# A decoder step on one core: page numbers looked up once per turn, and forget sums spread by two matmuls

## The reference, cut to what matters

```python
# one short-convolution layer (A), then one layer of attention with forget values (B), on
# x_prompt (1, 512, 1024) and x_sample (8, 8, 1024); 16 heads of 64
k, v, f = split(rmsnorm(h) @ kv_w)              # shared keys, values, forget gates
logf = log_sigmoid(f + f_bias)
F_p = cumsum(logf_prompt, axis=1)               # (512, 16): the forget sums of the prompt
# prompt: s = q k^T / 8 + F[query] - F[key], causal, softmax, times v
# samples: the keys and values of 2048 old positions come from 16 pages of 128 rows,
k_past = cache_k[page_table].reshape(8, 2048, 16, 64)
v_past = cache_v[page_table].reshape(8, 2048, 16, 64)
# and the 8 new ones follow; the same attention over past and new
y = x + (o * silu(z)) @ b_w_out
```

## Time and profile before

| | us |
|---|---|
| median of 3 runs | 965.42 |
| lowest and highest | 959.49 and 969.38 |
| the profiled execution's own time | 968.43 |
| its span, first to last instruction | 966.6 |
| busy: PE, DVE, ACT, POOL | 852.6, 557.5, 342.4, 217.2 |
| mean granted TensorE clock, of full speed | 0.959 |

### The profile page before, as it was taken

The page is one execution under the profiler, slowest core; times in us unless marked ns, Lnnn a source line. Parts: engine busy times, 40 slices in busy tenths (PEclk is TensorE's granted clock), DMA queues, the critical chain, the costliest instruction groups (busy, mean ns, idle before and its releaser), DMA issues.

```text
span 966.6 us, 23640 instructions
## 1 busy us (share of the span) xinstructions
PE 852.6 (88%) x8516; PEld 707.5 (73%) x8516; DVE 557.5 (58%) x1039; ACT 342.4 (35%) x728; POOL 217.2 (22%) x130
## 2 busy tenths in 40 slices
PE   3899999999998997988787888887888878877998
PEld 2899999999997996756555656565556555654998
DVE  4745655555336355568485584684856746836632
ACT  4233333333025444252451442524514415235210
POOL 2233333331211032221322213203222132121000
PEclk8899999999999999899998998998999989989999
DMA  6232233323536463688998988998989889896212
GB/s 202 67 87 70 82 87 87 87 84 93 163 90 230 145 195 92 214 313 270 325 334 244 399 292 304 378 275 317 331 256 401 282 282 387 277 357 223 89 44 99
DMA packets 148482, 206.65 MB, mean 214 GB/s; under 512 B 10527, under 2 KB 93136, under 8 KB 147266
## 3 DMA queue, kind: packets, MB, share of 16 engines
q1 hardware_dynamic: 138802, 199.40, 61.6%
q10 hardware_dynamic: 9088, 4.46, 1.5%
q0 software_dynamic: 528, 2.10, 0.8%
HBM read 195.29 MB, written 10.63 MB: 213 GB/s over the span
## 4 chain that ended last, share of the span: by engine, by line
PE 54%; SPq 24%; issue 10%; DVE 7%; DMA 4%; ACT 1%; POOL 0%; DVEq 0%; ACTq 0%; POOLq 0%
PE psum L1293 31%; SPq L379 11%; PE psum L1319 9%; SPq L388 8%; PE psum L1450 4%; PE psum L1263 3%; SPq L396 2%; PE psum L1557 2%; DMA page_ring<-in_cache_k 2%; DVE page_ring L1067 1%; DMA w_raw<-in_a_w_in 1%; DMA w_raw<-in_a_w_out 1%; PE psum L1490 1%; PE psum L1512 1%; PE psum L1367 1%
## 5 line engine op out<-in xcount | busy, mean ns | idle before, releaser
L1293 PE MATMUL psum<-xn_high,w_high 128*128 128x256 f32 x992 | 230.4, 314 | 45.2 <-DVE page_ring L1067 42.3
L1293 PEld LDWEIGHTS psum<-xn_high,w_high 128*128 128x128 f32 x992 | 167.8, 193 | 79.3 <-DVE page_ring L1067 45.8
L1293 PE MATMUL psum<-xn_low,w_high 128*128 128x256 f32 x992 | 216.0, 300 | 0.0
L1293 PE MATMUL psum<-xn_high,w_low 128*128 128x256 f32 x992 | 215.5, 299 | 0.0
L1067 DVE STREAM_TRANSPOSE page_ring<-page_ring 128x1024 f32<-128x1024 f32 x128 | 153.4, 1224 | 32.8 <-DMA page_ring<-in_cache_k 31.2
L1293 PEld LDWEIGHTS psum<-xn_low,w_high 128*128 128x128 f32 x992 | 170.5, 193 | 0.0
L1293 PEld LDWEIGHTS psum<-xn_high,w_low 128*128 128x128 f32 x992 | 170.4, 193 | 0.0
L551 POOL TENSOR_TENSOR w_raw<-w_raw,gains 128x1024 f32<-128x1024 f32 x32 | 61.6, 1927 | 275.3 <-DMA w_raw<-in_b_w_in 244.0
L913 DVE TENSOR_TENSOR w_low<-w_raw,w_high 128x1024 fp32r<-128x1024 f32 x32 | 54.1, 1692 | 74.5 <-ACT w_high L629 74.5
L1450 PE MATMUL psum<-page_ring,q_current 32*32 32x512 f32 x2048 | 84.1, 700 | 0.0
L528 POOL TENSOR_TENSOR w_raw<-w_raw,gains 128x1024 f32<-128x1024 f32 x30 | 60.8, 2027 | 89.6 <-DMA w_raw<-in_a_w_in 89.6
(11 more groups left out here) (243 smaller groups left out, 1429.8 us busy)
## 6 DMA issues: line engine op xcount, KB each, us to landing
page_ring<-in_cache_k SPq DMA_DIRECT2D x256, 256.0 KB, 4.1
page_ring<-in_cache_v SPq DMA_DIRECT2D x128, 512.0 KB, 6.5
w_raw<-in_a_w_in SPq DMA_DIRECT2D x32, 512.0 KB, 4.0
sample_scores<-suffix_scratch SPq DMA_DIRECT2D x8, 1024.0 KB, 9.6
w_raw<-in_b_w_in SPq DMA_DIRECT2D x16, 512.0 KB, 5.1
w_raw<-in_kv_w SPq DMA_DIRECT2D x16, 512.0 KB, 5.9
w_raw<-in_a_w_out SPq DMA_DIRECT2D x4, 1024.0 KB, 4.9
f_broad<-f_scratch SPq DMA_DIRECT2D x8, 512.0 KB, 4.1
```

The lines of the kernel that those rows point to most:

```text
L1293: mm = pe.matmul(PS[:, bank + h, 0:c.stop - c.start], w[:, k, :], x[:, k, c], start=(k == 0 and n == 0), stop=(k == KT - 1 and n == 2))
```

## The change

The diff has two parts.

1. SP reads the page numbers of a sample once: 16 calls of page_of at the head of a turn, kept in 16 registers, from which both halves of the keys and the values take their addresses. For that, the loop is cut in another place: its body is now "look up the pages of sample i + 1, load its keys, load its values", so that keys and values share the registers. The first sample's pages are looked up ahead of the loop. The order of the DMAs is otherwise kept, except that the last turn's new_bias load stands after the residual loads.
2. The broadcast DMA into f_broad is gone. PE opens each turn with two matmuls, [16 x 128] times [16 x 512] each: the weights (head_rows, SEL) are a row of the identity repeated in 128 columns, which picks one head of f_sum, and the result is that head's forget sums on all 128 partitions, in banks T0 and T1. ACT copies them to f_broad at the head of its turn. POOL makes SEL for the next turn (`select`). FT moves from f_broad's place to new_keys'. PE waits for POOL (b_sel) ahead of the two matmuls and for ACT (b_fb) ahead of past_scores(0); ACT waits for PE (b_fbp).

```diff
-        def load_keys(b, n, free=None):
-            pages = [page_of(b, 2 * (n % 8) + e) for e in range(2)]
+        def load_keys(pages, n, free=None):
             if free:
                 sp.wait_ge(*free)
             for e in range(2):
-                src = kpages[bass.ds(pages[e], 1), :, n // 8 * HALF_D:(n // 8 + 1) * HALF_D]
+                src = kpages[bass.ds(pages[2 * (n % 8) + e], 1), :, n // 8 * HALF_D:(n // 8 + 1) * HALF_D]
...
-        def load_values(b, n, free=None):
-            page = page_of(b, n)
-            if free:
-                sp.wait_ge(*free)
-            src = vpages[bass.ds(page, 1), :, :]
+        def load_values(pages, n):
+            src = vpages[bass.ds(pages[n], 1), :, :]
...
+        first = [page_of(0, n) for n in range(NPG)]
         sp.wait_ge(s_cs, H)
...
-        sp.dma_start(f_dram, FT[:, :]).then_inc(s_fst, 16)
+        sp.dma_start(f_dram[:, SEQ:TOK], FT[:, SEQ:TOK]).then_inc(s_fst, 16)
...
-        def heads(i, last):
-            sp.wait_ge(b_c0f, 4 * i)
-            sp.wait_ge(b_c1f, 4 * i)
-            src = f_dram[bass.ds(2 * i, 2), 0:SEQ].unsqueeze(0).to_broadcast([P, 2, SEQ])
-            sp.dma_start(FB[:, :, :], src).then_inc(b_fb, 16)
+        def values(pages, i, last):
             if not last:
                 sp.wait_ge(b_split, KT + 3 * i + 1)
                 load_w(wkv, (i + 1 + KT) * P, 0)
             for n in range(NPG):
-                load_values(i, n, (b_scored, 2 * i + n // 8 + 1) if n % 8 == 0 else None)
+                if n % 8 == 0:
+                    sp.wait_ge(b_scored, 2 * i + n // 8 + 1)
+                load_values(pages, n)
...
+        def next_turn(i, last):
+            pages = [page_of(i + 1, n) for n in range(NPG)]
             for n in range(NPG):
+                load_keys(pages, n, (b_used, NPG * i + n + 1))
                 if n == 8:
                     sp.wait_ge(b_t0, 8 * i + 4)
                     sp.wait_ge(b_t1, 8 * i + 4)
+                    load_suffix(i + 1)
+                if n == 13:
                     sp.wait_ge(b_split, KT + 3 * i + 5)
                     load_w(wqz, (i + 1 + KT) * P, 1)
+            values(pages, i + 1, last)
+        values(first, 0, False)
+        with sp.Fori(0, NB - 2) as i:
+            next_turn(i, False)
+        next_turn(NB - 2, True)
...
# POOL, once and then in every turn after the copy of the queries
+        def select(i):
+            rows2 = CT[0:H, bass.ds(C_ID + 2 * i, 2)].unsqueeze(2).to_broadcast([H, 2, P])
+            pool.tensor_copy(SEL[:, :, :], rows2).then_inc(b_sel, 1)
...
+                pool.wait_ge(b_fbp, i + 1)
+                select(i + 1)
# ACT, first in its turn
+            act.wait_ge(b_c0f, 4 * i)
+            act.wait_ge(b_c1f, 4 * i)
+            act.wait_ge(b_fbp, i + 1)
+            act.activation(FB[:, :, :], PS[:, T0:T0 + 2, :], ACT.Copy).then_inc(b_fb, 1)
# DVE
-            dve.wait_ge(b_fb, 16 * (i + 1))
+            dve.wait_ge(b_fb, i + 1)
# PE, first in its turn
+            pe.wait_ge(b_t0f, 8 * i)
+            pe.wait_ge(b_t1f, 8 * i)
+            pe.wait_ge(b_sel, i + 1)
+            for e in range(2):
+                mm = pe.matmul(PS[:, T0 + e, :], SEL[:, e, :], FT[:, 0:SEQ], start=True, stop=True)
+            mm.then_inc(b_fbp, 1)
             project(0, range(KT - 1))
             pe.wait_ge(b_qc, 16 * (i + 1))
-            pe.wait_ge(b_t0f, 8 * i)
-            pe.wait_ge(b_t1f, 8 * i)
+            pe.wait_ge(b_fb, i + 1)
```

More of the change, by code:

```diff
@@ L219, in build @@
     FL = place("f_log", [H, TOK], over=at["probs"])
-    FT = place("f_sum", [H, TOK], over=at["f_broad"])
+    FT = place("f_sum", [H, TOK], over=at["new_keys"])
+    SEL = place("head_rows", [H, 2, P], over=at["new_keys"] + 4 * TOK)
     SN = place("new_scores", [P, NB, NS], over=at["new_keys"])
@@ L271, in build @@
     b_fb, b_nbs, b_es, b_lp, b_sot = (
-        sem("f_broad_loaded"), sem("sample_bias"), sem("sample_exp"), sem("sample_sum"), sem("sample_out"))
+        sem("f_broad_ready"), sem("sample_bias"), sem("sample_exp"), sem("sample_sum"), sem("sample_out"))
     b_nbp, b_ep, b_pn, b_po, b_sz, b_gf, b_gh, b_gl = (
@@ L283, in build @@
         sem("gated_sl"), sem("past_weight"))
+    b_fbp, b_sel = sem("f_broad_made"), sem("head_rows_ready")
     s_hld = sem("h_loaded")
@@ L405, in _ @@
         sp.wait_ge(s_rows, 16 * 9)
+        first = [page_of(0, n) for n in range(NPG)]
         sp.wait_ge(s_cs, H)
         for n in range(2):
-            load_keys(0, n)
+            load_keys(first, n)
         for t in range(NT):
@@ L438, in _ @@
             if n < KT + 1:
-                load_keys(0, 5 + n)
+                load_keys(first, 5 + n)
             if n == KT:
                 sp.wait_ge(b_proj, 2)
-                load_keys(0, 14)
-                load_keys(0, 15)
+                load_keys(first, 14)
+                load_keys(first, 15)
         sp.wait_ge(s_fnr, 1)
@@ L462, in heads @@
                     load_w(wkv, (i + 1) * P, 1)
-            if last:
-                sp.wait_ge(b_split, KT + 3 * NB)
-                load_slab(wo_b, 0)
+        def next_turn(i, last):
+            pages = [page_of(i + 1, n) for n in range(NPG)]
             for n in range(NPG):
[L468 to L473, removed]
+                load_keys(pages, n, (b_used, NPG * i + n + 1))
                 if n == 8:
@@ L477, in heads @@
                     sp.wait_ge(b_t1, 8 * i + 4)
[L478 to L483, removed]
+                    load_suffix(i + 1)
+                if n == 13:
                     sp.wait_ge(b_split, KT + 3 * i + 5)
                     load_w(wqz, (i + 1 + KT) * P, 1)
-        with sp.Fori(0, NB - 1) as i:
-            heads(i, False)
-        heads(NB - 1, True)
+            values(pages, i + 1, last)
[3 more added lines that the diff above has]
+        next_turn(NB - 2, True)
+        sp.wait_ge(b_split, KT + 3 * NB)
+        load_slab(wo_b, 0)
+        for t in range(NT):
+            sp.wait_ge(b_used, NPG * (NB - 1) + t + 1)
+            sp.dma_start(X2[0:rows(t), t, :], h_dram[t * P:t * P + rows(t), :]).then_inc(s_hld, 16)
+        sp.wait_ge(b_t0, 8 * (NB - 1) + 4)
+        sp.wait_ge(b_t1, 8 * (NB - 1) + 4)
+        sp.dma_start(NBI[:, :, :].rearrange("p b n -> p (b n)"), table[:, C_NM:C_NM + NB * NS]).then_inc(b_nm, 16)
         sp.wait_ge(b_t1f, 8 * NB)
@@ L556, in _ @@
         pool.tensor_copy(QT[:, :], QF[:, 0, 0:SEQ]).then_inc(b_qt, 1)
+        def select(i):
+            rows2 = CT[0:H, bass.ds(C_ID + 2 * i, 2)].unsqueeze(2).to_broadcast([H, 2, P])
+            pool.tensor_copy(SEL[:, :, :], rows2).then_inc(b_sel, 1)
+        pool.wait_ge(s_st, 1)
+        select(0)
         def low_b(n, slot):
```

## The result

| | before | after |
|---|---|---|
| median, us | 962.45 (958.03 to 969.38) | 933.64 (930.4 to 946.28) |
| after / before, 95% interval | | 0.9699 [0.962, 0.9777] |
| span of the profiled execution, us | 966.6 | 944.4 |
| mean granted TensorE clock | 0.959 | 0.964 |

The kernel is 3% faster, by 29 us; I had forecast 40 (965 to 925).

What follows compares the result with a forecast made beforehand. SP's DMA issues and look-ups were taken to bound each turn, with PE next. Seven turns save 41.3 us and the last past_scores(1) 1.5, together 42.8 from 968.4: 925.6, called 925 us; range 917 to 944.

Steps and rivals of the forecast that it cites:

- The turn of 58.5 us: One past_scores(1) to the next: PE's 56.84 us without waits for keys, plus 1.7 for the new matmuls, makes 58.5.
- Seven turns: 450.8 - 7 x 58.5 = 41.3 us: Turns 0 to 6 together: 450.8 us measured before, each turn becoming 58.5, saves 41.3 us.
- The matmul pair: 1.7 taken: PE at the turn's head: two float32 matmuls of 512 columns add 1.6 to 1.8 us, taken as 1.7.
- ACT's copy at nothing: ACT's copy of the forget sums from PSUM, 1.06 us, falls near free time and costs nothing, at most 0.5 us.
- Rival D: PE waits for ACT's copy into f_broad, 1 us or so in each of 7 turns: 932 us. Chance 0.07.
- Look-ups at 0.58 us: SP's turn: each look-up costs 0.58 us; 48 a turn become 16, 27.8 us become 9.3, removing 18.5.
- These 21 us are the cover: PE frees the sixteen slots over 21.4 us, more slowly than SP issues, so SP's grouped look-ups are covered.
- The loop's end counted as moved, at no gain: SP's loop end, 3.8 us of issue, now stands between the values and the next sample's look-ups; no saving was counted.
- Rival A: Transfers bind next; the queue may run dry 6 to 7 us before slot 0's keys: turn 61 us, 944.6 us. Chance 0.2.
- Rivals B: SP stays the bound: the 1.16 us between slots is the queue's pace, only f_broad's issue goes: 963 us. Chance 0.04.
- C: Slower: holding 16 page numbers makes each DMA's address dearer; at 0.5 us each, turn 69, time 1000 us. Chance 0.03.
- The short waits ... come from DVE's softmax steps, which nothing here touches: PE's short waits inside the attention blocks come from DVE's softmax steps and stay in the 56.84 us turn.

Runs made afterwards that it cites:

- Experiment 4: The kernel after with f_sum and head_rows on 128 partitions, added ones zero, so the broadcast matmuls use 128 rows: 925.81 us, 0.9577 of before.
- Experiment 10: Experiment 4 with the 16 look-ups at the turn's head done twice, 9.3 us of SP more: 980.05 us, 1.0129 of before.
- experiment 3: The kernel after, unaltered, run again as the yardstick of its group: 937.76 us, 0.9626 of before.
- 2: The kernel after, with its matmuls and new loop cut, but a look-up ahead of each DMA, 48 a turn: 947.36 us, 0.9776 of before.
- 7: The kernel before with only the forget sums changed to matmuls, its old loop and 48 look-ups kept: 959.51 us, 0.9928 of before.
- 5: The kernel after with the 16-row matmul pair moved behind the first three eighths of the projection: 928.94 us, 0.96 of before.
- 1: The kernel after with f_broad by the DMA of before, so only the look-ups and the loop's new cut are changed: 926.78 us, 0.9572 of before.
- 6: The kernel after with POOL's two low parts waiting until DVE has done the softmax step beside which they ran: 917.81 us, 0.9502 of before.
- 8: The kernel after with both 128-row broadcast matmuls and POOL's low parts held until DVE's softmax steps are done: 918.47 us, 0.9415 of before.
- experiment 9: The kernel after with f_broad by the DMA of before and POOL's low parts held until DVE's softmax steps are done: 924.07 us, 0.9556 of before.

## Why the prediction was right, and where it was off

The range held the time (933.64 in 917 to 944), and so did the mechanism in the main: SP's issues bounded the turn, and now PE does. Which part of SP's work counted was off, and that the total came out within 9 us is partly luck, as errors of opposite sign stand in it.

- **The turn of 58.5 us: right at full clock.** 58.4 was measured. The step that failed is the multiplication by seven. "Seven turns: 450.8 - 7 x 58.5 = 41.3 us" took the clock of one turn for all; the profiled execution's seven took 433.6, 24 us above 7 x 58.5, all of it in turns at 0.89 and 0.94. Its own time is the longest of the four, so it overstates this: by the medians 8.6 us are missing. Against it stand the 4.3 us ahead of the turns, which I had not forecast. I had seen that the turn of 61.70 us, from which 56.84 came, was the only one shown that ran at 1.00 throughout, and should have kept a term for the fall.
- **What makes the falls long: 16 rows in the matmuls at the turn's head.** In none of the long falls do the matmuls start it. In the turn of the pair at 438.19 the clock falls some 2 us ahead of it, in the last attention block, behind the wait of 1.73 us, and it is back only at about 446.4:
```profile
434.00:435.80 1.80, 0.91 (x11) 0.56 (x14) 1.80 (x3) 0.52 (x3) 0.75 (x1) 1.00 1.06 328
435.80:438.10 2.30, 2.30 (x24) 0.63 (x16) 2.30 (x5) 2.10 (x9) 0.00 (x0) 0.56 1.01 198
...
446.80:450.00 3.20, 3.20 (x26) 3.20 (x26) 0.00 (x0) 0.00 (x0) 0.00 (x0) 1.00 1.11 341
```
Experiment 4 has the same fall, behind a wait of 1.64 us and 1.4 us ahead of its pair, and there, with 128 rows, the clock is back as the pair ends:
```profile
499.79 3.01 PE L1480 MATMUL psum<-f_sum,head_rows 128*128 128x512 f32 x4
498.30:500.60 2.30, 2.30 (x13) 0.89 (x14) 2.30 (x3) 2.08 (x10) 0.00 (x0) 0.54 1.15 287
...
502.20:510.00 7.80, 7.80 (x82) 6.85 (x81) 4.82 (x6) 1.03 (x1) 0.00 (x0) 1.00 1.02 319
```
Experiment 10, with 128 rows too, has one like it (the clock low from 708.0 to 711.5, the pair at 709.76). Ten low stretches of 10 us stand in the profiles with the 16-row pair at the head (three in after, four in experiment 3, two in 2, one in 7); in each the clock fell 1.6 to 3 us ahead of the pair, and the pair ran at the lower level (3.8 us); nine make the turns at 0.89. With 128 rows (4), another place (5), no pair (1) or POOL held off (6) none is over 4 us. (Before and experiments 8 to 10 have some of 7 us around past_scores(1), where PE waits for slots.) Seven of the nine turns come from two executions, the ones of 946.28 and 952.77 us, but the mean clocks of all executions say the same: 0.957 to 0.976 in the twelve of the changed kernel, 0.978 to 0.98 in five of six with 128 rows, 0.976 to 0.987 in all six with the other place. For the median it is only indicated: the intervals of experiments 3 and 4 overlap (0.9574 to 0.9678, 0.9525 to 0.9629).
- **The matmul pair: 1.7 taken, 1.91 measured** at the upper level. By my own row's most (0.91 for 576 columns) I should have stayed at 1.8.
- **ACT's copy at nothing: right.** ACT's timeline in after:
```profile
442.01 1.02 ACT L760 ACTIVATE f_broad<-psum 128x1024 f32<-128x1024 f32 x1 [1.73 <-PE psum L1479]
```
In this turn at the lower level ACT had crossed its loop's end and stood waiting. In the turn at the upper level whose pair starts at 564.97 it still had its queries and the past's output to copy and began the copy of the sums at 567.69, 0.8 us behind the pair; it was ready at 568.71, and past_scores(0) began at 573.47. Either way the loop's end cost ACT nothing to be seen, and PE has no wait for f_broad. Rival D is out.
- **Look-ups at 0.58 us: right in price, wrong in cover.** From the last value to the first key SP takes 20.6 us in experiment 10 and 11.4 in experiment 4, 9.2 for 16, 0.57 each. "These 21 us are the cover" counted PE's uses of the slots; experiment 10 shows that the cover is the backlog of the queue, 11 us. SP does catch up there (nine slots of keys in 9.97 us, 11.83 in experiment 4), but the transfers that were missed don't: their share is 1.00 over the next 36 us, and 9.3 us of SP cost nearly 8 a turn. It came out at nothing because the value DMAs went out earlier than I put them (590.03 is 4.5 us behind its past_scores(1), I took 6.2) and the loop's end took about 2 us there, not 3.8.
- **The loop's end counted as moved, at no gain: wrong.** Between experiments 7 and 2 only the cut of the loop differs, and the ratio falls from 0.9928 to 0.9776, 15 us. The look-ups then give 7 to 15 more (from 0.9776 to 0.9626 on the same chip, to 0.9699 in the first result). So half or more of the gain that I gave to the look-ups alone came from where the loop is cut. This error, the cover and the clock partly cancel in the total.
- **Rival A, the transfers: not in this kernel, but close.** Its floor, "57.3 / 1.05 = 54.6", is where experiment 8's best turn stands (55.1 at 1.05), and its queue that runs dry is what experiment 10 shows. The figure of about 358 GB/s that the prediction cites from the Trainium skill ("DMA: Bandwidth & Descriptors", section "Where 436 GB/s comes from") doesn't bind here: 389 to 406 GB/s stand in windows of several microseconds, 370 over a whole turn.
- **Rivals B and C: wrong.** Values go out eight in 3.7 us, 0.47 each, no dearer than before, and key slots stand 1.1 us apart where SP doesn't wait (ten DMAs in 5.45 us), no longer 1.7.
- **"The short waits ... come from DVE's softmax steps, which nothing here touches"**: true of the change, but it hid that POOL makes them. That was the next 1.2% to be had (experiment 6 against 3: 0.9502 against 0.9626).
- **Part 2: a small gain that depends.** Alone 0.9928; on top of part 1 at best nothing (0.9626 against 0.9572, intervals overlapping), since PE pays 1.9 us a turn for matmuls where it saves about 2.3 of waits for slots (16.1 over seven turns), and its 16 rows cost clock. Once POOL is held off, it pays a little: 0.9502 and 0.9415 against 0.9556 in experiment 9, though the intervals of 6 and 9 just overlap.

## What to carry to other kernels

When a sequencer bounds a turn, count its loads and its loop's end like work, and move them to where its DMA queue has a backlog; the cover here was what that backlog took to drain, not how long the consumer worked. A turn's time at full clock is a floor: multiply by it only when a row shows that all turns hold that clock. Where matmuls with few rows stand behind waits, try zeros up to 128 rows, or a place inside dense work; both helped here. Before calling an engine's small steps given, compare one instruction's time beside POOL with its time alone.

## What was not expected of the hardware

- When the clock had fallen just ahead of two float32 matmuls of 512 columns, it stayed at the lower level for 10 us in all ten cases with 16 rows, and for under 4 us in the two with 128 (experiments 4 and 10); turns of 64.5 to 64.8 us stand against 58.1 to 60.8 in experiment 4, with the same columns and passes. Why the rows matter was not measured.
- A DVE instruction of 0.16 us took 1.49 and 1.82 beside POOL's.
- One turn may fall in one execution and hold in the next of the same kernel: turn 2 stood at 1.00 in one profile and at 0.89 in the other, while turns 0, 1 and 3 stood at 0.89 in both.
- What spreads experiment 8's times over 19 us stays open.
